# Hybrid layer on Trainium2: the two scan streams cut into smaller steps, with loads, prologues and the spatial tiles moved

## The reference, cut to what matters

```python
ys = (gated_deltanet(...), spatial_gating(...), rwkv7_time_mix(...), native_sparse_attention(...))
gates = jnp.split(jax.nn.sigmoid(merge), N_MIXERS, axis=-1)
mixed = gates[0] * (ys[0] @ w_branch[0])
for i in range(1, N_MIXERS):
    mixed = mixed + gates[i] * (ys[i] @ w_branch[i])
return x + mixed @ w_out
```

## Time and profile before

| | us |
|---|---|
| median of 3 runs | 5059.65 (5056.14 to 5061.51) |
| profiled execution | 5054.45 |
| its span in the trace | 5052.6 |
| TensorE busy | 4310.3 |
| VectorE busy | 1996.7 |
| ScalarE busy | 1249.4 |
| GpSimd busy | 1197.7 |

### The profile page before, as it was taken

The page is one execution under the profiler, slowest core; times in us unless marked ns, Lnnn a source line. Parts: engine busy times, 40 slices in busy tenths (PEclk is TensorE's granted clock), DMA queues, the critical chain, the costliest instruction groups (busy, mean ns, idle before and its releaser), DMA issues.

```text
span 5052.6 us, 48929 instructions
## 1 busy us (share of the span) xinstructions
PE 4310.3 (85%) x19930; PEld 3413.1 (68%) x19930; DVE 1996.7 (40%) x2453; ACT 1249.4 (25%) x1569; POOL 1197.7 (24%) x584
## 2 busy tenths in 40 slices
PE   5546799999679999979999968988878886899877
PEld 4434588888556666758888857876767675766666
DVE  5883312222442222141222255215455553356452
ACT  2433221111212223222111132222122211145411
POOL 3552322222311111332222232221111110022133
PEclk9777899999779999989999979999989897789888
DMA  3001011111100000201111112221011102022142
GB/s 115 25 25 50 30 46 50 48 49 50 55 21 17 17 17 18 78 25 50 50 46 50 46 63 84 92 88 48 32 59 44 38 32 97 30 101 66 53 183 84
DMA packets 77417, 275.15 MB, mean 54 GB/s; under 512 B 8836, under 2 KB 9480, under 8 KB 72712
## 3 DMA queue, kind: packets, MB, share of 16 engines
q1 hardware_dynamic: 77192, 272.02, 15.3%
HBM read 219.55 MB, written 52.43 MB: 54 GB/s over the span
## 4 chain that ended last, share of the span: by engine, by line
PE 69%; DVE 20%; ACT 4%; POOL 3%; DMA 2%; issue 1%; SPq 0%; DVEq 0%; POOLq 0%; ACTq 0%
PE ps L349 45%; PE ps L378 6%; DVE ca L699 3%; PE ps L1296 2%; PE ps L1280 2%; DVE t L464 2%; PE ps L1962 2%; PE ps L1974 1%; PE ps L2817 1%; PE ps L1298 1%; PE ps L1969 1%; DVE inv L1992 1%; DVE ps L523 1%; DVE xlo L486 1%; DVE inv L1990 1%
## 5 line engine op out<-in xcount | busy, mean ns | idle before, releaser
L295 POOL TENSOR_TENSOR wlo<-wraw,whi 128x1024 fp32r<-128x1024 f32 x301 | 727.8, 2418 | 2826.8 <-ACT whi L287 2820.7
L349 PE MATMUL ps<-xhi,whi 128*128 128x512 f32 x3024 | 977.7, 405 | 178.3 <-DVE xlo L486 74.2
L349 PE MATMUL ps<-xlo,whi 128*128 128x512 f32 x3024 | 956.3, 398 | 0.0
L349 PE MATMUL ps<-xhi,wlo 128*128 128x512 f32 x3024 | 954.6, 398 | 0.0
L287 ACT ACTIVATE whi<-wraw 128x1024 fp32r<-128x1024 f32 x301 | 318.9, 1060 | 1926.0 <-PE ps L349 1728.9
L349 PEld LDWEIGHTS ps<-xhi,whi 128*128 128x128 f32 x3024 | 570.6, 194 | 305.7 <-DVE xlo L486 86.0
L349 PEld LDWEIGHTS ps<-xlo,whi 128*128 128x128 f32 x3024 | 584.0, 193 | 126.3
L349 PEld LDWEIGHTS ps<-xhi,wlo 128*128 128x128 f32 x3024 | 582.6, 193 | 125.5
L523 DVE TENSOR_TENSOR ps<-ps,t 128x1024 f32<-128x1024 f32 x161 | 198.5, 1233 | 1081.9 <-PE ps L349 1080.0
L378 PE MATMUL ps<-xhalf,whi 128*128 128x512 f32 x1024 | 393.4, 468 | 4.0 <-POOL wlo L295 4.0
L349 PE MATMUL ps<-xhalf,whi 128*128 128x512 f32 x1024 | 286.4, 403 | 33.0 <-DVE xhalf L486 21.2
(11 more groups left out here) (499 smaller groups left out, 5283.7 us busy)
## 6 DMA issues: line engine op xcount, KB each, us to landing
wraw<-in_w_dram SPq DMA_DIRECT2D x301, 512.0 KB, 3.5
g_keep<-gates SPq DMA_DIRECT2D x64, 256.0 KB, 2.4
gb<-g_keep SPq DMA_DIRECT2D x32, 512.0 KB, 5.2
p_keep<-stage SPq DMA_DIRECT2D x30, 512.0 KB, 2.9
x_keep<-x SPq DMA_DIRECT2D x12, 1024.0 KB, 3.8
x<-x_keep SPq DMA_DIRECT2D x8, 1024.0 KB, 8.0
x<-in_x_dram SPq DMA_DIRECT2D x4, 1024.0 KB, 12.8
n<-p_keep SPq DMA_DIRECT2D x8, 512.0 KB, 6.9
```

The costliest lines, as they stand in the source:

```text
L295: ge.own().tensor_tensor(K.lo(c), K.raw[:, c % NRAW, :], K.hi(c).bitcast(F32), SUB).then_inc(*K.G(("lo", c)))
L349: done = mm(into[a][:, h, :], wt, x[h], start=(i == 0 and j == 0), stop=(i == n - 1 and j == 2), skip_group_check=True)
```

## The change

```diff
-        b = take(pe, K, Q, n, "tt", k)
         pe.wait_ge(*K.at(n, "x", k))
         pe.wait_ge(*K.at(n, "tt", k - 1))
-        for i in range(4):
-            d = mm(K.ps[:, b, part(i)], I.X[:, part(i)], I.TT[:, part(i)], start=True, stop=True, skip_group_check=True)
-        d.then_inc(*K.T((n, "tt mm", k)))
         if k < 6:
             b = take(pe, K, Q, n, "t", k)
...
+        b = take(pe, K, Q, n, "tt", k)
+        for i in range(4):
+            d = mm(K.ps[:, b, part(i)], I.X[:, part(i)], I.TT[:, part(i)], start=True, stop=True, skip_group_check=True)
+        d.then_inc(*K.T((n, "tt mm", k)))
+        yield
...
+GDN_FIRST, GDN_BODY, GDN_NORM = 11, INVERSE_STEPS + 1 + 8, 7
...
             b = take(pe, K, Q, n, "ds", i)
...
+            yield
             pe.wait_ge(*K.at((n, "b1"), "rows"))
             pe.wait_ge(*K.at(n, "vn", i))
...
+    def body(j, q):
+        n = ("gdn", j, q)
+        if (j, q) != UNITS[-1]:
+            yield from wait_steps(2)
+            for s in range(2):
+                sy.wait_ge(*K.at(((n, s), "c"), "pairs mm"))
+            sy.wait_ge(*K.at(n, "qi"))
+            sy.wait_ge(*K.at(n, "ko in"))
+            sy.wait_ge(*K.at((n, "vt"), "turned"))
+            load(*UNITS[UNITS.index((j, q)) + 1])
+            yield from wait_steps(GDN_BODY - 2)
...
+SPATIAL_STEPS = 13
...
+def spatials(stream):
+    return rounds(stream(0), in_turn(wait_steps(1), stream(1)))
...
+RWKV_FIRST, RWKV_BODY, RWKV_NORM = 12, INVERSE_STEPS + 1 + 8, 9
...
+def spatial_gone(e, K):
+    for j in range(2):
+        e.wait_ge(*K.at(("sg", j), "kept"))
...
-RIGHT_LATER = 15
+RWKV_LATER = 3
...
-    scan_streams(in_turn(gdn_tensor(pe, K, QA, H, g[0]), spatial_tensor(pe, K, QA, H, s[0]), gdn_tensor(pe, K, QA, H, g[1]), spatial_tensor(pe, K, QA, H, s[1]),
-                         nsa_tensor(pe, K, QA, H, R.nsa)),
-                 in_turn(rwkv_tensor(pe, K, QB, H, w[0]), rwkv_tensor(pe, K, QB, H, w[1])), gates)
+    weave_beside(gates, in_turn(gdn_tensor(pe, K, QA, H, g), nsa_tensor(pe, K, QA, H, R.nsa)),
+                 in_turn(spatials(lambda j: spatial_tensor(pe, K, QB, H, s, j)), wait_steps(RWKV_LATER), rwkv_tensor(pe, K, QB, H, w)))
```

More of the change, by code:

```diff
@@ L2129, in gdn_vector @@
         yield
+        for s in range(2):
+            ve.wait_ge(*K.at((n, s), "d exp"))
+            ve.own().tensor_tensor(v4(B.DT[s]), v4(B.DT[s]), four(K.upper), MUL).then_inc(*V())
+            ve.wait_ge(*K.at(((n, s), "a"), "pairs mm"))
+            ve.own().tensor_tensor(B.inv[s].AT, K.bank(((n, s), "a"), "pairs"), B.DT[s], MUL).then_inc(*V(("free", (((n, s), "a"), "pairs"))))
+        attention(n, 0)
+        yield
+        attention(n, 1)
+        for s in range(2):
+            inverse_first(ve, K, H, ((n, s), "inv"), B.inv[s])
         if q == 0:
@@ L2212, in gdn_scalar, with norm @@
-        yield from rounds(head(0), head(1))
-        for i in range(4):
-            se.wait_ge(*K.at(n, "o mm", i))
-            se.own().activation(B.O[:, part(i)], K.bank(n, "o", i)[:, 0:128], ACT.Copy).then_inc(*S((n, "o kept"), ("free", (n, "o", i))))
-            yield
-        square_scalar(se, K, (n, "rs o"), B.O, B.Qn)
+    def norm(j, q):
+        n = ("gdn", j, q)
+        square_scalar(se, K, (n, "rs o"), B.O, B.last_sq)
+        yield from wait_steps(5)
+        back_scalar(se, K, (n, "rs o"), B.last_rs)
@@ L2218, in gdn_scalar, with first @@
         yield
-        back_scalar(se, K, (n, "rs o"), B.Kn)
         yield
+    yield from units(first, body, norm)
 def gdn_gpsimd(ge, K, H, B):
-    for q in range(2):
-        n = ("gdn", B.j, q)
-        for m in range(2):
-            sums_gpsimd(ge, K, (n, "rs", m), B.rows[m])
-        yield from wait_steps(4)
+    def first(j, q, before):
+        n = ("gdn", j, q)
+        yield from wait_steps(2)
+        sums_gpsimd(ge, K, (n, "rs"), B.rows)
+        yield from wait_steps(5)
+        if before:
+            ge.wait_ge(*K.at(("gdn", *before), "o mm", 3))
@@ L2443, in rwkv_tensor, with norm, masked, first @@
             yield
-        yield from head_norm_tensor(pe, K, Q, H, n, B.O, B.AL, (n, "o kept", 3))
+    def norm(j, q):
+        n = ("rw", j, q)
+        spread_tensor(pe, K, Q, (n, "mean"), H.heads, B.O, (n, "o kept", 3))
+        yield from wait_steps(3)
+        sums_tensor(pe, K, Q, H, (n, "rs o"), B.last_sq)
+        yield from wait_steps(3)
+        back_tensor(pe, K, Q, (n, "rs o"), B.last_sq)
+        yield from wait_steps(3)
+    yield from units(first, body, norm)
 def rwkv_vector(ve, K, H, B):
-    j, V, W = B.j, K.V, B.way
+    V, W = K.V, B.way
     tmp, Cs, AL, BE, KA, RO, Aa, Vv = B.tmp, B.Cs, B.AL, B.BE, B.KA, B.RO, B.Aa, B.V
-    for q in range(2):
+    def masked(n, s, what, dst, mask, *events):
+        hn = (n, s)
+        ve.wait_ge(*K.at((hn, what), "pairs mm"))
+        ve.own().tensor_tensor(v4(dst), v4(K.bank((hn, what), "pairs")), four(mask), MUL).then_inc(*V(("free", ((hn, what), "pairs")), (hn, what, "masked"), *events))
+    def first(j, q, before):
         n = ("rw", j, q)
+        if before:
+            ve.wait_ge(*K.at(("rw", *before), "o mm", 3))
+        else:
+            spatial_gone(ve, K)
         ve.wait_ge(*K.at(n, "in"))
@@ new lines, in rwkv_gpsimd, with first, norm, rwkv_load @@
+def rwkv_gpsimd(ge, K, H, B):
+    def first(j, q, before):
+        yield from wait_steps(3)
+        sums_gpsimd(ge, K, (("rw", j, q), "kk"), B.rows)
+        yield from wait_steps(RWKV_FIRST - 3)
+    def norm(j, q):
+        yield from wait_steps(4)
+        sums_gpsimd(ge, K, (("rw", j, q), "rs o"), B.last_rows)
+        yield from wait_steps(RWKV_NORM - 4)
+    yield from units(first, lambda j, q: wait_steps(RWKV_BODY), norm)
+def rwkv_load(sy, K, B, j, q):
+    bring(sy, K, B.way.into, (("rw", j, q), "in"), *((dst, K.keep_p[14 + 4 * j + k][:, HALVES[q]]) for k, dst in enumerate((B.KA, B.RO, B.V))))
```

683 lines of the change are left out of this document (383 added, 300 removed).

## The result

The changed kernel takes 4855.32 us (4 runs, 4847.67 to 4862.66), the kernel before on the same chip 5060.58: a ratio of 0.959, 95% interval 0.9566 to 0.9614, 205 us. The forecast was 4955 (4885 to 5035); the gain is about twice the one predicted.

The account below looks back on a forecast made before the run. TensorE, busy 85% of the span, was taken as the bound, its idle time lying mostly in the scans. Terms -150 +30 +48 -20 -12 = -104 took 5054.45 to 4950, plus 5.2 for the runs' median: 4955 us, range 4885 to 5035.

Parts of the forecast that it names:

- Waits removed, -150 +30: In the scans, 150 us of TensorE's 209.1 us idle go; bank takes in the new prologue and other waits add 30.
- t/tt: In the inversions, the fourth matmul group's wait for a bank falls from 39.4 to 2 us with t issued before tt.
- the start of the inversion: In the scans, moving its two VectorE operations ahead of the transposes cuts their wait from 22.6 to 2 us.
- the early loads: In the scans, loads of units 2 to 4 issued in the body, 20 steps early, cut 21.0 us of waits to 2.
- Waits are moved, not removed: Rival for the whole kernel: t/tt saves half, clock and attention give nothing, takes cost 50; 5027 us (4995 to 5050), chance 0.20.
- Gate steps, +48: 47 gate steps move from the attention to the scans at 1.03 us each, costing 48 us there (40 to 57).
- theory G: Follow-up theory: gate steps in the scans hold the clock up and fill waits; e3 0 to 30 us faster, e4 0 to 20 slower.
- C: Follow-up theory that the clock follows the waits; for e4, clock stays at 0.91, about 13 us faster than the changed kernel.
- Clock, -20: In the scans, less idle time raises TensorE's granted clock, giving back 20 us (0 to 60).
- Attention, -12: With 47 gate steps gone the attention gets 12 us shorter (0 to 30), since gates in its late rounds were nearly free.
- the clock pays more: Rival: the scans stay at clock 0.95 or above, clock term -60, the prologue's takes cost nothing; 4890 us, chance 0.15.
- VectorE late at every step: Slow rival: late VectorE operations hold TensorE in 156 small steps of prologues and norms; 5081 us at 1.0 each, chance 0.09.

Follow-up runs that it names:

- e5: Changed kernel with norm and next prologue one behind the other, every eighth gate step beside the scans skipped; ratio 0.9574 to the kernel before.
- e14: Changed kernel with six parts undone: tt first, norm then prologue, late unit loads, late NSA loads, inversion start with its transposes, state step in one; 0.9782 of before.
- e1: Kernel before with only t issued ahead of tt in each inversion cycle; ratio 0.9909 to the kernel before, 45 us faster.
- e7: Changed kernel with the loads of units 2 to 4 asked for at the end of the former unit's body; ratio 0.9602 to the kernel before.
- e13: e5 with the loads of units 2 to 4 asked for when the former unit's result is out; ratio 0.9605 to the kernel before.
- e15: Changed kernel with norm then prologue, norms in 2 and 3 steps, unit loads after the former result; ratio 0.9605 to the kernel before.
- e3: Kernel before with a second gate step after every sixth beside the scans, 47 more there; ratio 0.9983 to the kernel before, 9 us faster.
- e4: Changed kernel with every seventh gate step beside the scans left to the attention; ratio 0.9634 to the kernel before.
- e2: Changed kernel with tt issued ahead of t again; ratio 0.9682 to the kernel before.
- e6: Changed kernel with GpSimd and SP counting 23 steps for a body instead of 22; ratio 0.9586 to the kernel before.
- e10: Changed kernel with the two VectorE operations that start an inversion back in the step of its transposes; ratio 0.9606 to the kernel before.
- e9: Changed kernel with NSA's loads asked for after delta net's last norm instead of seven steps before its end; ratio 0.9619 to the kernel before.

## Why the prediction was wrong, step by step

- **Waits removed, -150 +30.** Mis-sized by 20 us: -140 in all, 162 removed and 22 added. Of the named rows t/tt came out at 1.8 (2 taken), the start of the inversion at 4.2 (2), the start's load at 13.2 with its low weight chunk (16), softmax at 11.2 (12.9), bonus and vn at 0.5 and none (1 each). (The smaller rows before were ten, not nine; their sum of 38 was right.) The bank takes of the new prologue are the 22.0 us of L2018, in the range of 20 to 52; without the rounds of norm and prologue 3.9 are left in e5 and 12.5 in e14, so the rounds hold them in part. "Waits are moved, not removed" is thereby out.

  Two of the reasons were wrong where the number was right. The prediction said that the cover of t and tt is TensorE's own work and does not depend on the other stream. In e1 the same order of instructions still waits 13.2 us there, 9 times, and in the kernel after 1.8. What it waits for is VectorE's subtraction, so the cover also hangs on what else VectorE has to do in that arrangement. And it gave 21.0 us to the early loads. Asked for late again they cost 1 us by the medians beside the rounds (e7) and 10 to 15 without them (e13, e15), and in none of these does TensorE wait for delta net's loaded squares; 3.4 of the 21.0 were norms' squares in the first place.
- **Gate steps, +48.** The count was right (331 of 335). The work of 46 more is 37 us at full speed (e3: 37.5 for 47), 40 at the clock after: the lower end of 40 to 57. What was missed is that the scans then wait less and run at a higher clock; the whole effect on the scans was 32 us in e3 and 18 in e4. (By the theories on record: my own terms fell in e3 and theory G's time held; in e4 C fell, and G's 0 to 20 held at its edge.)
- **Clock, -20.** Mis-sized, by 25 us. At the clock before, the 762.1 us of work after would have taken 762.1/0.877 = 869; they took 823.4: -45. The estimate gave the idle share its say and then held back for NSA's stretch. e14 gives back 26 us of it with six parts; e1 and e2, with 29 and 30 us of waits less and more, leave the clock where it was. So the clock does not follow the microseconds of wait one by one, and what set it is not isolated.
- **Left out: the work of the other matmuls.** Work grew by 13.6 us though the gates brought 37, so 23 went elsewhere (by a measure that is good to a few us). The prediction had no term for it: it priced a wait at itself, and a break also costs overlap and a slower start, 10 us by e1, 12 by e2. The other half is not isolated; the delta net's sums took 18.8 us at 324 ns before, where they stood behind waits, and 11.3 at 247 ns after, for the same 96 matmuls.
- **Attention, -12.** Mis-sized, by 21 us in this trace and by 28 against the 328 us of four others, and here the argument was faulty. The first operations of n = 5, 6 and 7 on VectorE after, against 4644.40, 4693.21 and 4746.03 before:

```profile
4477.78 1.23 DVE L3032 SCALAR_TENSOR_TENSOR n<-ps,n 128x512 f32<-128x512 f32 x2 [2.22 <-PE ps L3003]
...
4517.35 1.36 DVE L3032 SCALAR_TENSOR_TENSOR n<-ps,n 128x512 f32<-128x512 f32 x2 [0.77 <-PE ps L3003]
...
4564.69 0.69 DVE L3032 SCALAR_TENSOR_TENSOR n<-ps,n 128x512 f32<-128x512 f32 x1 [1.72 <-PE ps L3003]
```

  and of the kernel before, the one that the earlier trace rows leave out:

```profile
4644.40 1.23 DVE L2834 SCALAR_TENSOR_TENSOR n<-ps,n 128x512 f32<-128x512 f32 x2 [2.22 <-PE ps L2805]
```

  n = 5 lost 9.2 us (9 said), n = 6 5.5 (0 to 11 said), but n = 7 went from 53.3 to 41.6, where -2 to 3 was said. That two rounds of unlike gate load last equally long was read as proof that gates are free in both; in n = 7, though, 19.04 us were y matmuls at the lower level. After, the same 88 take 10.04, and the slow stretch stands a round earlier:

```profile
4545.48 17.17 PE L3015 MATMUL ps<-n 128*128 128x64 f32 x80
4595.71 10.04 PE L3015 MATMUL ps<-n 128*128 128x64 f32 x88
```

  This slow stretch belongs to the one execution that was traced. In e7, whose attention is the same, the 80 matmuls take half the time:

```profile
4547.34 9.14 PE L3001 MATMUL ps<-n 128*128 128x64 f32 x80
```

  So they do in e2, e6 and e10. In those traces n = 6 loses some 15 us instead of 5.5 (38.1 left of 52.8 in e7), and with that the argument on n = 6 (0 to 11) fails too. e3 and e4 settle the term without any of this: 47 steps are 33 to 40 us of the attention.
- **The sum.** The terms that failed are thus the clock's size, the attention's argument and the work beside the waits, which had no term. Waits 20 better, clock 25, work left out 23, gates 8, attention 21: 97 us, against the 88 by which -192 misses -104; the 9 us are the later end of the projections. No single rival held this; "the clock pays more" had the right side and half the size. VectorE late at every step did not happen.
- The page's rule cited in the prediction (the Trainium skill, TensorE: Matmul & The Clock Gate, "A second HAM failure mode: psum-queue depth-cycling") would have left the clock term at 0, as the prediction read it. The trace does not bear that reading out: matmuls that still cycle through three banks a way ran at 0.926 instead of 0.877. The section names the short idles between the groups as well, and those became fewer; that much agrees.

What was argued after the result and fell: that the rounds of norm and prologue, or the early loads, brought the gain (e5, e7, e13); that every microsecond of wait taken out brings half a microsecond of busy time (e9 has 11.0 us of wait back and 3 of busy time).

## What to carry to other kernels

Price a wait inside a series of small matmuls at its length plus what the break costs, and count breaks, not only microseconds; a single long wait was worth little more than itself (e9). When work moves from one stage to another, measure its price in both by adding and removing just that work: here 47 steps were worth 33 to 40 us where they left and 18 to 32 where they came. When a wait may have several covers, taking each away alone can show next to nothing (the inversion's start: 8.8 us of wait alone, 17.3 and 24.8 with others gone), so undo them together before calling one of them useless. Compare single parts on one chip and with enough runs: effects of 5 to 10 us were inside the noise here. And before a reason is read from one trace, look at a second trace of the same code: 8 us of the attention were one execution's own.

## What the runs showed of the hardware that was not expected

A stretch at the lower clock level can begin 1 to 2 us behind a short wait. In TensorE's timeline after, the 16 matmuls of a cycle behind a wait of 0.89 us take 3.17 us; the next 16 of such a step, at 3618.65, take 1.95. The granted clock is 1.00 in 3610 to 3612, 0.57 in 3612 to 3616 and 1.00 again in 3616 to 3620.

```profile
3610.69 1.16 PE L2018 MATMUL ps<-g 64*128 64x128 f32 x8 [0.89 <-DVE g L2178]
3611.77 0.95 PE L378 MATMUL ps<-xhalf,whi 128*128 128x512 f32 x2
3612.52 0.63 PE L378 MATMUL ps<-xhalf,wlo 128*128 128x512 f32 x1
3612.95 3.17 PE L1965 MATMUL ps<-inv 128*128 128x128 f32 x16
3615.88 0.71 PE L378 MATMUL ps<-xhalf,whi 128*128 128x512 f32 x2
3616.43 0.40 PE L378 MATMUL ps<-xhalf,wlo 128*128 128x512 f32 x1
```

The low weight matmul shows the two levels, 0.63 us ahead of the slow step and 0.40 behind it. It does not follow every wait (the 0.61 us of the earlier trace rows has none behind it). And it can come without one: nine microseconds earlier TensorE had run on without idle time, and eight matmuls that take 1.06 us in the earlier trace rows took

```profile
3601.71 1.77 PE L1973 MATMUL ps<-inv 128*128 128x128 f32 x8
```

No run here says what decides. The same code does not decide it either: ahead of the 80 y matmuls of n = 6 the granted clock is 0.50 in the kernel after and in e7, for the same instructions with the same waits; in e7 it is 1.00 as they start, and in the kernel after it stays at 0.50 for 20 us more.

More matmuls in the same time can be cheaper than their own duration: the 47 gate steps of e4's difference are 33.1 us of work, and the scans were 17.9 us shorter without them, with 5.6 us more of waits and a clock of 0.911 instead of 0.926.
